# An encoder block with 32 experts: one 1 MB weight chunk brought in 16 transfers of 8 partitions each

## The chip, the cores and the metric

The kernel runs on one core of a Trainium2 chip. The metric is the time of one execution on the device in microseconds (us); lower is better. The input is one sequence of 256 tokens with a width of 1024, all in float32.

## What is computed

One encoder layer: RMSNorm, a combined projection, three token mixers (neighbourhood attention, dilated windows, attention to a memory), their gated merge with a residual, and then the expert stage, in which the change lies. Each token goes to 4 of 32 experts. Cut to what matters:

```python
logits = h @ router_w + router_b
top_val, top_idx = lax.top_k(logits, 4)
top_w = softmax(top_val)
# per expert e, for the tokens xb that chose it:
gu = xb @ w_gu[e] + b_gu[e]              # w_gu[e]: 1024 x 2048
g = minimum(gu[:, :1024], 7.0)
u = clip(gu[:, 1024:], -7.0, 7.0)
a = (u + 1.0) * (g * sigmoid(1.702 * g))
y = a @ w_dn[e] + b_dn[e]                # w_dn[e]: 1024 x 1024
# x += sum over the chosen experts of top_w * y, then a last RMSNorm
```

## The kernel before, in words

The front (the mixers) takes about the first quarter of the time. Then all 32 experts are worked through in order, each with a block of up to 64 gathered tokens; tokens beyond that would go through an overflow loop. Each expert's weights, 12 MB, are read once from the chip's main memory and used once.

**Chunks and the ring.** Weights come in chunks of 1 MB: 128 partitions x 8 KB (CHUNK = 2048 floats). An expert has 12 (EXPERT_CHUNKS): chunks 0 to 7 are gate/up, 8 to 11 down. They lie in a ring of 20 slots (RING) in the arena, chunk c in slot c % 20. In the source, a partition's part of one gate/up chunk is one piece of 8 KB, and neighbouring chunks follow each other, so that a transfer of m chunks has one run of m x 8 KB in each partition.

**The order of the transfers** is worked out by transfers() (lines 156 to 171). Each entry is (expert, first chunk, number of chunks). Experts 4 to 30 take the list long, (0, 4) and (4, 4): two transfers of 4 MB for gate/up. Down comes as two transfers of 2 MB. The first three experts and the last take smaller ones, and expert 6 has a list of its own with four transfers of 1 MB, because three of its chunks are put at other places (LENT). In the order, the gate/up chunks of expert n stand ahead of the down chunks of expert n - 1.

**Who issues.** SP issues all transfers, in the loop at lines 543 to 554: before each it waits until TensorE has used the chunks that lay in the slots (line 546), then load_weights (line 443) issues one transfer, at line 450, which raises the semaphore of its ring slot by 16.

```python
sp.wait_ge(chunk_used, NF + c - RING + m)
load_weights(*TRANSFERS[c], ring_slot(c))
```

**Who waits.** TensorE goes through an expert at lines 948 to 994: a small product for the bias, then the gate/up products of chunks 0 to 7 (gate_up, matmuls of line 591), between them the scatter of the expert before last and the transposes of line 898 (after chunk 3) and the gathering of later tokens (after chunk 5), then the down products of expert n - 1 and the transposes of line 904. Ahead of the first chunk of each transfer it waits in weights_landed (line 932) until the semaphore of the slot has come to 16 for each fill so far; fills_through (line 400) counts the fills. All matmuls are recorded at line 591, all weight transfers at line 450. gate_up and down raise chunk_used after each chunk.

VectorE and ScalarE take the products out of PSUM and compute the activation; GpSimd has no work in this stage.

Of the kernel before, what the change touches and what calls it, by code (L numbers as in the profile page):

```python
# [25 lines left out]
P = 128  # L26
# [13 lines left out]
EXPERTS, TOP_K = 32, 4  # L40
# [7 lines left out]
CHUNK = 2048  # L48
# [7 lines left out]
EXPERT_CHUNKS = 12  # L56
# [42 lines left out]
FIRST_LONG = 4  # L99

LENT_TO = 6
LENT = tuple(EXPERT_CHUNKS * LENT_TO + j for j in (1, 2, 3))

QK_DONE, QKV_DONE = {"C": 6, "A": 10, "B": 18}, {"C": 6, "A": 12, "B": 21}
# [41 lines left out]
def gate_up_chunk(n):  # L146

    return EXPERT_CHUNKS * n - 4 if n else 0
# [7 lines left out]
def transfers():  # L156

    short, long, down = [(j, 2) for j in range(0, KC, 2)], [(0, 4), (4, 4)], [(KC, 2), (KC + 2, 2)]
    end_down = [(KC, 2), (KC + 2, 1), (KC + 3, 1)]
    first_down = [(KC, 1), (KC + 1, 1), (KC + 2, 2)]  # L160
    order = [(0, 0, 2), (0, 2, 2), (0, 4, 2), (0, 6, 1), (0, 7, 1)]
    for n in range(1, EXPERTS):
        lent = [(0, 4), (4, 1), (5, 1), (6, 1), (7, 1)]
        order += [(n, *t) for t in (lent if n == LENT_TO else long if FIRST_LONG <= n < EXPERTS - 1 else short)]
        order += [(n - 1, *t) for t in (first_down if n == 1 else down if n < EXPERTS - 1 else end_down)]
    order += [(EXPERTS - 1, *t) for t in end_down]
    c, out = 0, {}
    for e, j, m in order:
        out[c] = (e, j, m)
        c += m  # L170
    return out


TRANSFERS = transfers()


# [4 lines left out]
def build(nc, t):  # L181
# [4 lines left out]
    w_gu = t["expert_w_gate_up"].rearrange("l e (p a) c -> (l e) p (a c)", p=P)  # L186
# [5 lines left out]
    with ExitStack() as ctx:  # L192
# [3 lines left out]
        def sem(name):  # L196
            return ctx.enter_context(nc.semaphore(name))
# [25 lines left out]
        ring = arena[:, 0:RING * CHUNK].rearrange("p (r c) -> p r c", r=RING)  # L223
# [105 lines left out]

        landed = [sem(f"landed{i}") for i in range(RING)]  # L330
        lent_in = {c: sem(f"lent_in{c}") for c in LENT}
        sums_open, overflow_added = sem("sums_open"), sem("overflow_added")
        first_in, t5_in_done, consts_in = sem("first_in"), sem("t5_in_done"), sem("consts_in")
        mem_in = [sem(f"mem_in{i}") for i in range(T)]
# [47 lines left out]
        def ring_slot(c):  # L382

            return c % RING

        def front_fills(r):

            return len(range(r - FRONT_SLOT, NF, FRONT_RING)) if FRONT_SLOT <= r < FRONT_SLOT + FRONT_RING else 0

        x_flat = x[:].rearrange("p t c -> p (t c)")  # L390
        bias_flat = bias_raw[:].rearrange("p b c -> p (b c)")
        lent_pieces = {LENT[2]: [behind_work[:, 512 * i:512 * (i + 1)] for i in range(4)],
                       LENT[0]: [bias_flat[:, 0:512], bias_flat[:, 512:1024], until_ranked[:], until_routed],
                       LENT[1]: [x_flat[:, 512 * i:512 * (i + 1)] for i in range(4)]}

        def piece(c, i):

            return lent_pieces[c][i] if c in LENT else ring[:, ring_slot(c), 512 * i:512 * (i + 1)]

        def fills_through(c):  # L400

            return front_fills(ring_slot(c)) + sum(ring_slot(b) == ring_slot(c) for b in TRANSFERS if b <= c and b not in LENT)

        ALL_CHUNKS = EXPERTS * EXPERT_CHUNKS

        def overflow_fills(j):

            return front_fills(ring_slot(j)) + sum(ring_slot(c) == ring_slot(j) for c in TRANSFERS if c not in LENT) + 1

        def by_row(dst, tt):  # L410

# [30 lines left out]
        def _(sp):  # L442
            def load_weights(e, j, m, r):

                if j < KC:
                    src = w_gu[bass.ds(e, 1), :, j * CHUNK:(j + m) * CHUNK].rearrange("o p c -> (o p) c")
                else:
                    first = (j - KC) % 2 * CHUNK
                    src = w_dn[bass.ds(e, 1), :, (j - KC) // 2, first:first + m * CHUNK].rearrange("o p c -> (o p) c")
                sp.dma_start(ring[:, r:r + m, :].rearrange("p r c -> p (r c)"), src).then_inc(landed[r], 16)  # L450

            def lend(c, first, n, place):

                e, j, _ = TRANSFERS[c]
                src = w_gu[bass.ds(e, 1), :, j * CHUNK + 512 * first:j * CHUNK + 512 * (first + n)].rearrange("o p c -> (o p) c")
                sp.dma_start(place, src).then_inc(lent_in[c], 16)
# [5 lines left out]
            for i in range(NF):  # L462
# [7 lines left out]
                kind, n = FRONT[i]  # L470
                dst = raw_of(i)
                if i in WIDE_FIRST or i in WIDE_LAST:
                    late = int(i in WIDE_LAST)
                    first = (n - late) * SLOTS_W
                    src = {"mem": w_mem, "in": w_in}[kind][:, 4 * late:4 * late + 4, first:first + 2 * SLOTS_W]
                    dst = dst.rearrange("p (k c) -> p k c", k=4)
                elif kind in ("mem", "in", "out"):
                    src = {"mem": w_mem, "in": w_in, "out": w_out}[kind][:, :, n * SLOTS_W:(n + 1) * SLOTS_W]
                    dst = dst.rearrange("p (k c) -> p k c", k=KC)
                elif kind == "branch_b":  # L480
                    src, dst = w_br[kind], dst.rearrange("p (k c) -> p k c", k=2)
                else:
                    src, dst = w_br[kind][:, :, n * 512:(n + 1) * 512], dst.rearrange("p (k c) -> p k c", k=4)
                if i == 0:
                    sp.dma_start(dst[:, 0:KC // 2], src[:, 0:KC // 2]).then_inc(first_half_in, 16)
                    dst, src = dst[:, KC // 2:], src[:, KC // 2:]
# [56 lines left out]
            for c, (_, _, m) in TRANSFERS.items():  # L543
                if c < RING or c in LENT:
                    continue
                sp.wait_ge(chunk_used, NF + c - RING + m)
                load_weights(*TRANSFERS[c], ring_slot(c))
                if c == RING:
                    sp.wait_ge(routed, 1)
                    lend(LENT[0], 3, 1, until_routed)  # L550
                if c == gate_up_chunk(LENT_TO + 2):
                    assert c - RING + m > LENT[1]
                    sp.dma_start(b_dn, t["expert_b_down"].rearrange("l e c -> (l e) c")).then_inc(b_dn_in, 16)
                    sp.dma_start(final_g, bass.AP(t["final_norm_g"].tensor, 0, [[0, P], [1, D]])).then_inc(final_g_in, 16)
# [34 lines left out]
        def _(pe):  # L589
# [342 lines left out]
            def weights_landed(c):  # L932

                if c in LENT:
                    pe.wait_ge(lent_in[c], {LENT[0]: 48, LENT[1]: 16, LENT[2]: 16}[c])
                else:
                    pe.wait_ge(landed[ring_slot(c)], 16 * fills_through(c))

            def down_products(n, bank):

                pe.wait_ge(aT_ready, n + 1)
                for j in range(KC, EXPERT_CHUNKS):
                    c = down_chunk(n) + j - KC
                    if c in TRANSFERS:
                        weights_landed(c)
                    down(ring_slot(c), j, bank)

            for n in range(EXPERTS):
# [10 lines left out]
                for k in range(KC):  # L959
                    c = gate_up_chunk(n) + k  # L960
# [49 lines left out]
            with pe.If(0 < n_over):  # L1010
                with pe.Fori(0, MAX_OVERFLOW) as b:
                    with pe.If(b < n_over):
                        n = b + EXPERTS
                        pe.wait_ge(P_ready, b + (EXPERTS // 2 + 1))
                        for half in range(2):

                            pe.wait_ge(XT_ready, b * 2 + (EXPERTS + half))
                            gather_half(half, BLK)
                        pe.wait_ge(XT_ready, b * 2 + (EXPERTS + 2))
                        pe.wait_ge(pick_ready, b + (EXPERTS + 1))  # L1020
                        pe.wait_ge(gu_drained, n + 1)
                        bias_rows(1)
                        for k in range(KC):
                            if k % 2 == 0:
                                pe.wait_ge(landed[ring_slot(k)], (b + overflow_fills(k)) * 16)
                            gate_up(lambda i: piece(k, i), k, XT[:, 0, :, 0:BLK])
                            if k == 3:
                                pe.wait_ge(PW_ready, n + 1)
                                turn_weights()
                        pe.wait_ge(WT_ready, n + 1)  # L1030
                        pe.wait_ge(act_ready, n + 1)
                        turn_act()
                        pe.wait_ge(aT_ready, n + 1)
                        for j in range(KC, EXPERT_CHUNKS):
                            if j % 2 == 0:
                                pe.wait_ge(landed[ring_slot(j)], (b + overflow_fills(j)) * 16)
                            down(ring_slot(j), j, 3)
                        pe.wait_ge(y_ready, n + 1)
                        scatter(1, overflow_added)
# [587 lines left out]
```

## Time and profile before

| | |
|---|---|
| median of 3 runs | 1218.38 us (1218.35 to 1219.38) |
| the profiled execution | 1214.18 us |
| its span, first to last instruction | 1212.4 us |
| mean granted TensorE clock | 0.989 |
| TensorE busy | 1162.4 us, 96% |
| moved by DMA | 455.15 MB, mean 375 GB/s |

The profile is that of one execution; times inside it are counted from the start of its span. PE is TensorE, SP the engine that issues the transfers (SPq its queue). A wait is put down to what came last. Busy TensorE time includes the time in which a matmul waits inside the array's pipeline, so 96% is not 96% of the peak.

### The profile page before, as it was taken

The page shows a single profiled execution, that of the slowest core. Times are in us where ns is not written, and L with a number is a line of the kernel's source. Part 1 is how long each engine was busy: PE and PEld are TensorE (multiplying, and loading weights), DVE is VectorE, ACT ScalarE, POOL GpSimd, SP SyncE. Part 2 cuts the span into 40 slices and gives each one's busy share as a digit, 9 for nine tenths or more (in the row PEclk, how much of TensorE's full clock was granted, in tenths as well). Part 3 has the DMA queues.
Part 4 walks back from the last instruction along what each step waited for, and adds up shares of the span by engine and source line. Part 5 has one row for each costly group of instructions (what it writes and reads, how often), then busy time and mean ns, then how long its engine had stood idle before and what let it go on. Part 6 is the DMA issues. An engine that isn't in the chain of part 4 may idle for free.

```text
span 1212.4 us, 14185 instructions
## 1 busy us (share of the span) xinstructions
PE 1162.4 (96%) x6145; PEld 594.1 (49%) x6145; DVE 247.1 (20%) x511; ACT 269.5 (22%) x579; POOL 206.5 (17%) x89
## 2 busy tenths in 40 slices
PE   8999999999999999999999999998899989989996
PEld 8989877898434333333343333333333333333332
DVE  3136122233321121111111211111111111111112
ACT  6457567445110111001011100100000000000002
POOL 5865757785000000000000000000000000000000
PEclk9999999999999999999999999999999999999999
DMA  8766645587999999999999999999999999999995
GB/s 287 261 243 217 203 144 172 211 282 266 429 429 425 431 431 435 415 434 432 430 431 432 431 432 432 433 432 431 431 432 432 431 431 432 431 431 430 432 430 240
DMA packets 62136, 455.15 MB, mean 375 GB/s; under 512 B 5129, under 2 KB 33705, under 8 KB 43512
## 3 DMA queue, kind: packets, MB, share of 16 engines
q1 hardware_dynamic: 62072, 454.22, 90.5%
q8 instruction: 50, 0.82, 0.2%
q14 instruction: 14, 0.11, 0.0%
HBM read 453.13 MB, written 1.07 MB: 375 GB/s over the span
## 4 chain that ended last, share of the span: by engine, by line
PE 65%; DMA 30%; ACT 2%; DVE 1%; POOL 1%; issue 0%; DVEq 0%; SPq 0%; ACTq 0%; POOLq 0%
PE ps L591 62%; DMA arena<-in_expert_w_gate_up 26%; DMA arena<-in_expert_w_down 3%; PE ps L904 1%; PE ps L646 1%; PE ps L898 1%; ACT arena L1104 1%; POOL w_lowc L580 0%; ACT arena L1094 0%; POOL w_lowa L580 0%; DMA arena<-in_mem 0%; DVE arena L1394 0%; ACT L1118 0%; DVE arena L1398 0%; DVE arena L1406 0%
## 5 line engine op out<-in xcount | busy, mean ns | idle before, releaser
L591 PE MATMUL ps<-arena,gathered_T 128*64 128x512 f32 x2034 | 469.4, 609 | 31.8 <-DMA arena<-in_expert_w_gate_up 31.8
L591 PE MATMUL ps<-arena 128*64 128x512 f32 (+6 forms) x1490 | 316.4, 562 | 2.2 <-DMA arena<-in_expert_w_down 1.3
L591 PEld LDWEIGHTS ps<-arena,gathered_T 128*64 128x64 f32 x2034 | 144.3, 139 | 296.3 <-issue 269.3
L591 PEld LDWEIGHTS ps<-arena 128*64 128x64 f32 (+3 forms) x1490 | 113.4, 149 | 194.9 <-issue 192.3
L1227 ACT COPY arena<-ps 128x256 f32<-128x256 f32 x32 | 11.9, 372 | 350.2 <-PE ps L898 350.2
L1506 DVE TENSOR_SCALAR arena<-arena 128x128 f32<-128x128 f32 x64 | 19.3, 344 | 306.9 <-PE ps L898 306.9
L1512 DVE TENSOR_SCALAR arena<-ps 128x512 f32<-128x512 f32 x32 | 22.1, 692 | 275.1 <-PE ps L591 275.1
L1218 ACT ACTIVATE gathered_T<-ps,g_cols 128x128 f32<-128x128 f32 x128 | 36.6, 368 | 172.9 <-PE ps L591 172.9
L591 PEld LDWEIGHTS ps<-arena,x_normed 128*128 128x128 f32 x512 | 59.5, 191 | 24.8 <-issue 24.3
L591 PE MATMUL ps<-arena,x_normed 128*128 128x128 f32 x512 | 65.4, 281 | 0.2 <-DVE arena L1463 0.2
L1237 ACT COPY arena<-ps 128x512 f32<-128x512 f32 x31 | 18.2, 586 | 172.2 <-PE ps L591 172.2
L1521 DVE COPY arena<-ps 128x512 f32<-128x512 f32 x32 | 22.1, 692 | 154.9 <-PE ps L904 154.9
L580 POOL TENSOR_TENSOR w_lowa<-arena,w_high 128x1024 fp32r<-128x1024 f32 x20 | 48.9, 2470 | 22.8 <-ACT w_high L1074 13.7
L580 POOL TENSOR_TENSOR w_lowc<-arena,w_high 128x1024 fp32r<-128x1024 f32 x20 | 48.6, 2451 | 20.3 <-ACT w_high L1074 20.3
L580 POOL TENSOR_TENSOR w_lowb<-arena,w_high_odd 128x1024 fp32r<-128x1024 f32 x20 | 48.0, 2423 | 22.4 <-ACT w_high_odd L1074 22.4
L580 POOL TENSOR_TENSOR w_lowd<-arena,w_high_odd 128x1024 fp32r<-128x1024 f32 x20 | 47.5, 2399 | 19.1 <-ACT w_high_odd L1074 19.1
L1074 ACT CAST w_high_odd<-arena 128x1024 fp32r<-128x1024 f32 x40 | 39.9, 1047 | 32.8 <-PE ps L591 32.7
L1074 ACT CAST w_high<-arena 128x1024 fp32r<-128x1024 f32 x38 | 37.9, 1046 | 41.1 <-PE ps L591 41.0
L1231 ACT ACTIVATE arena<-arena 128x512 f32<-128x512 f32 x32 | 20.3, 633 | 108.8 <-DVE arena L1512 108.8
L591 PE MATMUL ps<-w_high_odd,h_T_parts 128*128 128x256 f32 (+1 forms) x240 | 41.5, 322 | 0.0
L591 PEld LDWEIGHTS ps<-w_high_odd,h_T_parts 128*128 128x128 f32 x240 | 34.5, 188 | 5.3 <-issue 1.4
L904 PEld LDWEIGHTS ps<-ident,arena 128*128 128x128 f32 x128 | 17.8, 208 | 26.0 <-issue 26.0
(229 smaller groups left out, 895.7 us busy)
## 6 DMA issues: line engine op xcount, KB each, us to landing
arena<-in_expert_w_gate_up SPq DMA_DIRECT2D x53, 4096.0 KB, 38.5
arena<-in_expert_w_down SPq DMA_DIRECT2D x61, 2048.0 KB, 38.6
arena<-in_expert_w_gate_up SPq DMA_DIRECT2D x19, 2048.0 KB, 10.6
arena<-in_w_in SPq DMA_DIRECT2D x29, 1024.0 KB, 5.1
arena<-in_expert_w_down SPq DMA_DIRECT2D x6, 1024.0 KB, 38.6
arena<-in_expert_w_gate_up SPq DMA_DIRECT2D x4, 1024.0 KB, 7.0
arena<-in_w_out SPq DMA_DIRECT2D x4, 1024.0 KB, 5.8
arena<-in_w_mem_kv SPq DMA_DIRECT2D x3, 1024.0 KB, 11.4
```

The source lines that it names most:

```text
L580: last = nc.gpsimd.tensor_tensor(low_of(i)[:, half], raw_of(i)[:, half], high_of(i)[:, half].bitcast(F32), ALU.subtract)
L591: return nc.tensor.matmul(out, lhsT, rhs, start=start, stop=stop, **kw)
L646: last = nc.tensor.transpose(ps[:, 6 + hh, kt * S + tt * P:kt * S + (tt + 1) * P], scores[:, u % 4, hh, tt, kt * P:(kt + 1) * P], ident[:])
L898: last = nc.tensor.transpose(ps[:, 3, tt * P:(tt + 1) * P], PW[:, tt, :], ident[:])
L904: last = nc.tensor.transpose(ps[:, 2, f * P:(f + 1) * P], sig.rearrange("p (q f) -> p f q", f=4)[:, f, :], ident[:])
L1074: nc.scalar.copy(high_of(i)[:, half], raw_of(i)[:, half]).then_inc(high_ready, 1)
L1218: last = nc.scalar.mul(xt[:, c, 0:width], ps[:, bank, k * P:k * P + width], g_cols[:, 3 * KC + c:3 * KC + c + 1])
L1231: nc.scalar.activation(sig, gate_c, ACT.Sigmoid, scale=ALPHA).then_inc(sig_ready, 1)
L1237: nc.scalar.copy(y_sb, ps[:, bank, :]).then_inc(y_ready, 1)
L1506: last = vec.tensor_scalar(PW[:, tt, :].rearrange("p (a s) -> p a s", a=2), bcast(slots, 1, 2), key_tile[:, tt, e], w_sel[:, tt, e], ALU.i ...
L1512: vec.tensor_scalar(gate_c, ps[:, 0, :], LIMIT, None, ALU.min).then_inc(gate_ready, 1)
L1521: vec.tensor_copy(aT, ps[:, 2, :].rearrange("p (f s) -> p f s", f=4)).then_inc(aT_ready, 1)
```

## The change

The second gate/up transfer of expert 24, (4, 4), becomes (4, 3) and (7, 1). The second of these, the last gate/up chunk (number EIGHTHS = 12 * 24 + 3 = 291), isn't brought by load_weights but by 16 transfers, each over 8 partitions with 8 KB in each, 64 KB. They raise a semaphore of their own, 256 in all, and TensorE waits for 256. The counts of fills of the ring slot leave this chunk out. Nothing else is changed.

```diff
+EIGHTHS_OF = 24
+EIGHTHS = EXPERT_CHUNKS * EIGHTHS_OF + 3
...
         lent = [(0, 4), (4, 1), (5, 1), (6, 1), (7, 1)]
-        order += [(n, *t) for t in (lent if n == LENT_TO else long if FIRST_LONG <= n < EXPERTS - 1 else short)]
+        eighths = [(0, 4), (4, 3), (7, 1)]
+        order += [(n, *t) for t in (lent if n == LENT_TO else eighths if n == EIGHTHS_OF else long if FIRST_LONG <= n < EXPERTS - 1 else short)]
...
+        eighths_in = sem("eighths_in")
...
-            return front_fills(ring_slot(c)) + sum(ring_slot(b) == ring_slot(c) for b in TRANSFERS if b <= c and b not in LENT)
+            return front_fills(ring_slot(c)) + sum(ring_slot(b) == ring_slot(c) for b in TRANSFERS if b <= c and b not in LENT and b != EIGHTHS)
...
                 sp.wait_ge(chunk_used, NF + c - RING + m)
-                load_weights(*TRANSFERS[c], ring_slot(c))
+                if c == EIGHTHS:
+                    e, j, _ = TRANSFERS[c]
+                    for p in range(0, P, 8):
+                        src = w_gu[bass.ds(e, 1), p:p + 8, j * CHUNK:(j + 1) * CHUNK].rearrange("o p c -> (o p) c")
+                        sp.dma_start(ring[p:p + 8, ring_slot(c), :], src).then_inc(eighths_in, 16)
+                else:
+                    load_weights(*TRANSFERS[c], ring_slot(c))
...
                 if c in LENT:
                     pe.wait_ge(lent_in[c], {LENT[0]: 48, LENT[1]: 16, LENT[2]: 16}[c])
+                elif c == EIGHTHS:
+                    pe.wait_ge(eighths_in, 16 * (P // 8))
                 else:
                     pe.wait_ge(landed[ring_slot(c)], 16 * fills_through(c))
```

## Rows read from the trace of the kernel before

**Rows 1.** The page's 40 slices of the span: TensorE and the DMA rate.
```profile
PE   8999999999999999999999999998899989989996
DMA  8766645587999999999999999999999999999995
GB/s 287 261 243 217 203 144 172 211 282 266 429 429 425 431 431 435 415 434 432 430 431 432 431 432 432 433 432 431 431 432 432 431 431 432 431 431 430 432 430 240
```

**Rows 2.** Busy time in a stretch of 100 us ahead of the first waits.
```profile
core 0: us, PE busy (x) PEld busy (x) DVE busy (x) ACT busy (x) POOL busy (x), PEclk, DMA share, GB/s
600.00:700.00 100.00, 100.00 (x478) 38.03 (x474) 17.02 (x39) 10.36 (x27) 0.00 (x0) 1.00 1.01 433
```

**Rows 3.** The chain, one expert, early: start, length, what.
```profile
361.88 0.37 PE ps L898 x2
...
388.34 0.37 PE ps L898 x2
```

**Rows 4.** TensorE's waits for transfers (total us, times, longest), whole span, then from 860 us.
```profile
PE ps L591 <- DMA arena<-in_expert_w_gate_up: 31.8, 25, 2.3
...
PE ps L591 <- DMA arena<-in_expert_w_gate_up: 19.4, 15, 2.3
```

**Rows 5.** TensorE's instructions in order of time, the last experts.
```profile
1141.62 8.78 PE L591 MATMUL ps<-arena,gathered_T 128*64 128x512 f32 x32 [2.26 <-DMA arena<-in_expert_w_gate_up]
1185.38 7.09 PE L591 MATMUL ps<-arena 128*64 128x512 f32 x32 [1.29 <-DMA arena<-in_expert_w_down]
```

**Rows 6.** Around the changed transfer: its issue, the chain, TensorE, SP's next issues.
```profile
933.37 0.33 SPq L450 DMA_DIRECT2D arena<-in_expert_w_gate_up  x1
...
933.37 42.66 DMA arena<-in_expert_w_gate_up
...
976.08 3.65 PE L591 MATMUL ps<-arena,gathered_T 128*64 128x512 f32 x16 [0.98 <-DMA arena<-in_expert_w_gate_up]
979.66 2.05 PE L591 MATMUL ps<-arena,x_normed 128*128 128x128 f32 x16
981.65 3.65 PE L591 MATMUL ps<-arena,gathered_T 128*64 128x512 f32 x16
...
941.98 3.76 SPq L450 DMA_DIRECT2D arena<-in_expert_w_down  x2
```

**Rows 7.** Two stretches in which expert 6's transfers of 1 MB are moved.
```profile
440.00:455.00 15.00, 15.00 (x78) 6.06 (x78) 3.41 (x7) 2.15 (x6) 0.00 (x0) 1.00 1.00 426
455.00:470.00 15.00, 15.00 (x72) 5.29 (x70) 2.08 (x8) 0.96 (x2) 0.00 (x0) 1.00 1.02 440
```

**Rows 8.** Issue times in ns and landing in us: weights, bias, output.
```profile
L450 SPq DMA_DIRECT2D arena<-in_expert_w_gate_up x75: 327/328/584, 44.6 to 1138.3; - x75
...
L525 SPq DMA_DIRECT2D bias_raw<-in_expert_b_gate_up x4: 580/599/732, 295.6 to 297.7; - x4
DMA to landing us min/median/max: 2.7/3.0/9.2
...
DMA to landing us min/median/max: 2.6/2.7/2.8
```

**Rows 9.** The page's packets and its transfers with rows of 8 KB or more.
```profile
DMA packets 62136, 455.15 MB, mean 375 GB/s; under 512 B 5129, under 2 KB 33705, under 8 KB 43512
q8 instruction: 50, 0.82, 0.2%
q14 instruction: 14, 0.11, 0.0%
arena<-in_expert_w_gate_up SPq DMA_DIRECT2D x53, 4096.0 KB, 38.5
arena<-in_expert_w_down SPq DMA_DIRECT2D x61, 2048.0 KB, 38.6
arena<-in_expert_w_gate_up SPq DMA_DIRECT2D x19, 2048.0 KB, 10.6
...
arena<-in_expert_w_down SPq DMA_DIRECT2D x6, 1024.0 KB, 38.6
```

More of the change, by code:

```diff
@@ L400, in fills_through @@
         def fills_through(c):
-            return front_fills(ring_slot(c)) + sum(ring_slot(b) == ring_slot(c) for b in TRANSFERS if b <= c and b not in LENT)
+            return front_fills(ring_slot(c)) + sum(ring_slot(b) == ring_slot(c) for b in TRANSFERS if b <= c and b not in LENT and b != EIGHTHS)
         ALL_CHUNKS = EXPERTS * EXPERT_CHUNKS
         def overflow_fills(j):
-            return front_fills(ring_slot(j)) + sum(ring_slot(c) == ring_slot(j) for c in TRANSFERS if c not in LENT) + 1
+            return front_fills(ring_slot(j)) + sum(ring_slot(c) == ring_slot(j) for c in TRANSFERS if c not in LENT and c != EIGHTHS) + 1
         def by_row(dst, tt):
```

## The prediction

> **What bounds the kernel now.** I read the page's slices first, then stretches of the expert stage, then the waits and the chain, and last the two queues around the edit. The reader is to see in the slices that TensorE and the DMA engines are both nearly full from about a quarter of the span on, and that the DMA rate stands at 430 to 435 GB/s there [rows 1]. So busy shares don't decide; the waits do. Up to about 700 us TensorE never waits for a transfer: a stretch of 100 us has 100 us of TensorE work [rows 2]. It needs 26.5 us for an expert (from one L898 group of the chain, at 361.88, to the next, at 388.34) [rows 3]. An expert brings 12 MB, 12 x 1024 x 1024 bytes = 12.58 million bytes, which takes 29.2 us at 431 GB/s. TensorE thus eats up the lead that the ring of 20 chunks gives it, and from then on it waits for gate/up transfers: all its waits for them come to 31.8 us in 25 waits, 19.4 us of that in 15 waits after 860 us [rows 4]. From there to the end the chain runs from one weight transfer to the next, and the last of them, a down transfer, lands at 1185 us with TensorE waiting 1.29 us [rows 5]. **The bound around expert 24 is the DMA stream**, and TensorE has 29.2 - 26.5 = 2.7 us to spare per expert.
>
> The transfer that is changed is the second gate/up one of expert 24, issued at 933.37 us and waited for until 976.04, 42.66 us later; TensorE stood still 0.98 us for it [rows 6]. It spends 4 MB at 431 GB/s = 9.7 us of its 42.7 us being moved; for the other 33 us it stands behind earlier ones. The queue is that deep, and it is never dry.
>
> **The change, part by part.** *The split of (4, 4) into (4, 3) and (7, 1).* No byte is added. The 3 MB part lands one chunk earlier, 1.05 MB / 431 GB/s = 2.43 us, which lets TensorE start chunk 4 earlier, but the end hangs on the bytes behind it: 0. The wait on the freed slots is split into one for 3 slots and one for the fourth: with 33 us of queue in front, 0. Elsewhere the kernel brings chunks as single 1 MB transfers (expert 6, the stretch 440 to 470 us), and the rate stays at 426 and 440 GB/s [rows 7], so the smaller size over all 128 partitions is no cost.
>
> *SP's 16 issues.* A weight transfer takes the queue 0.33 us to issue; the four loads of the bias took up to 0.73 [rows 8]. 16 of them are 5.3 to 11.7 us. Behind them on SP stand the two down transfers of expert 23, issued in this lap 8.6 us after the transfer in question (941.98) [rows 6]; so they go out between 0 and about 3.4 us late. Cover: 33 us of queued transfers. Cost 0; without that cover it would be those 3.4 us, once. TensorE's one wait for 256 instead of a ring slot's count costs nothing by itself. POOL has nothing in this stage.
>
> *The rows of each transfer.* This is the term that counts. Each packet is one partition's row: 53 transfers of 4 MB, 80 of 2 MB (61 of them down) and 12 of 1 MB with rows of 8 KB (six of w_down, four of w_gate_up, and two into x), times 128, are 18,560; with the 64 instruction packets of queues 8 and 14 that makes 18,624, and the page has 62,136 - 43,512 = 18,624 packets of 8 KB or more, exactly [rows 9]. Rows are not cut up. A transfer of 8 rows then has 8 packets, and at most 8 of the 16 engines work on it. The Trainium skill says the same and more (DMA: Bandwidth & Descriptors, section on why a DMA increments its semaphore by 16): it takes the largest count up to 16 that divides the outer dimension, on the lowest-numbered engines, so all 16 pieces would go to the same 8. No view here shows which engine a packet ran on.
>
> If it is the same 8 each time (another 8 now and then would make it less), each of them carries 16 rows of 8 KB (131 KB) where it would have carried 8 (66 KB). At 431/16 = 27 GB/s per engine this is 4.86 us instead of 2.43: **+2.4 us** on these 8. The other 8 go on to later transfers, but every later transfer has rows on all 16, so it lands with the late ones, and at a stream that is full to the end they don't catch up. That is the lower end for a loss, if the eight are as late as the rest before it; if they are ahead of the others, part or all is hidden (down to 0).
>
> The upper side: the eight engines write to 8 neighbouring partitions at the same time, where the transfers of before spread over 128. The nearest rows are the four loads of the bias, 128 KB into 32 partitions each, beside the two halves of the output, 512 KB over 128 partitions: 2.7 to 3.0 us to landing against 2.6 to 2.8 [rows 8]. A quarter of the bytes in a quarter of the partitions isn't faster at all. Most of that is a fixed latency, so the rows allow both readings: time by bytes, or time by bytes per partition. Taken to the end, the second reading makes each piece as long as a 1 MB transfer over all partitions, 2.43 us, and the 16 in a row 38.9 us, +36.5. That is the far end, and it has no overlap between pieces. I take a middle case: neighbours in fours share a path into the memory with the rate of one engine. In step, four engines then need 4 x 8.2 KB / 27 GB/s = 1.21 us per piece, 19.4 us for 16, +17.0. But the engines are not held in step, since each goes to its next row as soon as it is done; with two at a time on a path it is 0.61 us per piece, 9.7 us for 16: **9.7 - 2.43 = +7.3 us**. I take this one, between +2.4 and +17, because the engines have run freely for 700 us and will be spread. The Trainium skill has such a rule (SBUF — State Buffer, section on the DMA port swizzle): four neighbouring partitions share one of 16 ports, and a load into partitions 0 to 3 was measured at 27.6 GB/s, about a port's limit. By that page the in-step estimate of +17 is right for engines in lockstep. No run here shows it.
>
> *What the delay does.* TensorE reaches chunk 7 of expert 24 about 7.5 us after chunk 4 (two chunks of 3.65 us together, 2.05 us of gathering, one chunk of 1.8) [rows 6]; with a landing of 3 MB 2.4 us earlier it gets there near 981 to 984 us, so a delay up to 5 us isn't even seen there but in the down products of expert 23 and at expert 25. TensorE's pause may lower its clock for a while, as after the waits of over 2 us, where 32 matmuls take 8.78 us instead of 7.09 [rows 5]: 1.7 us, which the spare 2.7 us per expert cover. The tail after 1185 us is the same. So the sum is the delay of the stream, +7.3 us.
>
> The profiled execution took 1214.18 us beside a span of 1212.4; the median of the runs is 1218.38, 4.2 us above. I put the difference on the median: 1218.38 + 7.3 = 1225.7. About 0.2% (2.4 us) is what a measurement of this kernel can tell from no change.
>
> **Rivals.**
> - *Only the double load of eight engines* (no shared path): +2.4 us, 1220.8, with 1220.2 to 1221.3 for the spread of the engines. For it: the rate of a single engine is all that the rows prove. Against it: the bias loads. It stands just on the border of 0.2%. Chance 0.25.
> - *In step on the shared path, or worse*: +12 to +36, about 1235. Against it: nothing keeps the engines together. Chance 0.10.
> - *Not slower*: the eight engines that carry the small rows are those ahead of the others. The place is the landing of each transfer, which goes by its last engine; the price is zero as long as their lead is larger than 2.4 us (alone) or 7.3 us (shared path), and from that point on the rest shows. Also here: small transfers that do spread over all engines after all. 1218.4. Against it: eight of sixteen being all early is unlikely. Chance 0.12.
> - *Each small transfer pays its latency in turn*: 16 x 2.7 us = 43 us, +40. Against it: the queue holds several transfers at once, and single 1 MB transfers keep the full rate [rows 7]. Chance 0.02.
> - *Faster*: an earlier chunk 4 moves TensorE ahead; but the stream sets the end. Chance 0.03.
>
> **How the numbers follow.** The forecast, +4 to +11 us, has 0.48. The time is 1225.7. The range 1218.2 to 1231.0 takes in the hidden case, the double load, the forecast with its own range (1222.4 to 1229.4) and the low edge of the in-step case; it leaves out the rest of that, the latency in turn and most of the faster case, some 0.15. Slower by over 0.2%: 0.48, half of the double load (0.12), 0.10 and 0.02, 0.72 in all. Within 0.2%: the other half of that rival, 0.13, and the hidden case, 0.12, 0.25 in all. Faster: 0.03.
>
> **What the profile would show.** Right: expert_w_gate_up issues with 16 more of 64 KB and one of 3 MB; one dip in the DMA rate right around 970 to 1000 us and 431 GB/s again behind it; TensorE's waits for transfers up by about 7 us in all, first at expert 23's down products or at expert 25, with every later event shifted by one and the same amount up to the tail. Only a double load: the same with 2.4. Wrong: no shift before the tail (hidden), a shift that grows or shrinks after expert 26 (then the stream isn't the bound I take it for), or a late issue of the down transfers with the DMA share falling to nothing (SP's issues matter).

## The result and the profile after

The changed kernel takes 1226.3 us (median of 5 runs, 1223.05 to 1226.69) against 1218.35 us for the kernel before on the same chips (5 runs, 1216.04 to 1219.38): ratio 1.0063, 95% interval 1.0047 to 1.0078, or 7.7 us, with 5.7 to 9.5 as its interval. It is slower, and forecast was 1225.7.

The profiled execution was the one of 1226.3 us, with a span of 1224.5 us, 12.1 us more than the span before. The first lines to read are the page's slices and its packets, which answer to [rows 1, 9]:

```profile
PE   8999999999999999999999999999999979899996
DMA  8776645687999999999999999999999999999994
GB/s 286 264 243 200 205 144 172 211 287 268 427 431 428 430 438 432 415 430 435 434 428 432 434 433 430 430 432 429 432 430 431 373 402 434 430 434 429 433 428 184
DMA packets 62392, 455.15 MB, mean 372 GB/s; under 512 B 5257, under 2 KB 33833, under 8 KB 43640
```

The reader is to see two slices of 373 and 402 GB/s where 430 stood, while the DMA digit stays 9: the engines were as busy as ever and moved less. The page has 256 packets more. 128 of them are data (a 4 MB transfer had 128 rows; now there are 128 of 24 KB and 128 of 8 KB), the other 128 are small, under 512 B (5257 - 5129): 16 transfers with 8 semaphore updates each. That is one for each engine that carries a part, so 8 engines carry each transfer. The Trainium skill's rule (DMA: Bandwidth & Descriptors, section Why a DMA increments its semaphore by 16 and not by 1), the largest divisor up to 16, agrees with this trace: 8.

Around the event, in stretches of 10 us (columns: stretch, its length, busy time of PE, PEld, DVE, ACT, POOL with counts, granted clock, DMA share, GB/s):

```profile
960.00:970.00 10.00, 7.77 (x36) 2.89 (x34) 2.71 (x7) 0.58 (x1) 0.00 (x0) 0.95 0.99 422
970.00:980.00 10.00, 9.86 (x40) 3.52 (x36) 0.10 (x1) 0.10 (x1) 0.00 (x0) 0.88 1.00 239
980.00:990.00 10.00, 9.19 (x48) 3.98 (x48) 0.64 (x3) 1.41 (x5) 0.00 (x0) 1.00 1.02 356
990.00:1000.00 10.00, 8.14 (x40) 3.10 (x38) 2.75 (x5) 1.22 (x2) 0.00 (x0) 1.00 1.03 442
```

239 GB/s with a DMA share of 1.00 (the change's small rows begin at 969.2 us). A double load on eight engines alone can't do this: it moves work among engines, but each engine goes on at its own rate. Over the 30 us the mean is 346 GB/s, so bytes for (431 - 346) x 30 / 431 = 5.9 us were not moved.

Then TensorE, in order of time, which answers to [rows 6], with the start of expert 24 and of expert 25:

```profile
965.84 0.72 PE L601 MATMUL ps<-bias_parts,pick 128*128 128x512 f32 x2
968.79 8.78 PE L601 MATMUL ps<-arena,gathered_T 128*64 128x512 f32 x32 [2.23 <-DMA arena<-in_expert_w_gate_up]
...
980.81 3.65 PE L601 MATMUL ps<-arena,gathered_T 128*64 128x512 f32 x16 [0.95 <-DMA arena<-in_expert_w_gate_up]
984.39 2.05 PE L601 MATMUL ps<-arena,x_normed 128*128 128x128 f32 x16
986.38 3.65 PE L601 MATMUL ps<-arena,gathered_T 128*64 128x512 f32 x16
990.79 3.65 PE L601 MATMUL ps<-arena 128*64 128x512 f32 x16 [0.76 <-DMA arena<-in_expert_w_down]
995.55 3.65 PE L601 MATMUL ps<-arena 128*64 128x512 f32 x16 [1.10 <-DMA arena<-in_expert_w_down]
999.13 0.75 PE L914 MATMUL ps<-ident,arena 128*128 128x128 f32 x4
999.64 0.71 PE L601 MATMUL ps<-bias_parts,pick 128*128 128x512 f32 x2
1005.20 9.42 PE L601 MATMUL ps<-arena,gathered_T 128*64 128x512 f32 x32 [4.85 <-DMA arena<-in_expert_w_gate_up]
...
1195.79 7.09 PE L601 MATMUL ps<-arena 128*64 128x512 f32 x32 [1.31 <-DMA arena<-in_expert_w_down]
```

For chunk 7 itself, brought in 16 parts, TensorE doesn't stop (986.38 holds chunks 6 and 7). It stops 0.76 and 1.10 us at the two down transfers of expert 23 and 4.85 us at expert 25. In the trace of before, the rows at the same places of the program are:

```profile
965.73 7.09 PE L591 MATMUL ps<-arena,gathered_T 128*64 128x512 f32 x32 [0.91 <-DMA arena<-in_expert_w_gate_up]
...
985.13 7.04 PE L591 MATMUL ps<-arena 128*64 128x512 f32 x32
...
995.42 7.09 PE L591 MATMUL ps<-arena,gathered_T 128*64 128x512 f32 x32 [2.11 <-DMA arena<-in_expert_w_gate_up]
```

Taken at waits that a landing ended in both traces: at expert 24's first chunk the changed kernel is 968.79 - 965.73 = 3.1 us late already, before anything that was changed. At expert 25 it is 1005.20 - 995.42 = 9.8 us late, and at the last down transfer 1195.79 - 1185.38 = 10.4 us [rows 5]. **The event thus cost 6.7 to 7.3 us in these two executions, and it was kept to the end.** The other 3.1 us are the difference of these two executions ahead of expert 24 (the profiled one of before was 4.2 us under its median), and 1.7 us of the difference of the spans lie behind the last down transfer.

SP and its queue, answering to [rows 6, 8]:

```profile
937.82 6.92 SPq L555 DMA_DIRECT2D arena<-in_expert_w_gate_up  x16
944.79 0.54 SPq L454 DMA_DIRECT2D arena<-in_expert_w_down  x1
```

Beside these views, the trace keeps two kinds of records that are used below. A packet record has the start, the duration and the size of one DMA packet, and not its engine. A landing record has the time of each update that an engine, or the issuing queue, makes to a transfer's semaphore.

### The profile page after: what moved, and what is told of

Same layout as the page of the kernel before. It is cut to its first block, busy times and chain, and to the rows that moved or that the text cites. A ratio compares the mean times of both kernels' runs of the same rounds, so it can differ in the third digit from the quotient of the medians.

```text
span 1224.5 us, 14201 instructions
## 1 busy us (share of the span) xinstructions
PE 1169.4 (96%) x6145; PEld 597.5 (49%) x6145; DVE 246.5 (20%) x511; ACT 269.6 (22%) x579; POOL 206.0 (17%) x89
## 2 busy tenths in 40 slices
DMA packets 62392, 455.15 MB, mean 372 GB/s; under 512 B 5257, under 2 KB 33833, under 8 KB 43640
## 4 chain that ended last, share of the span: by engine, by line
PE 62%; DMA 34%; ACT 2%; DVE 1%; POOL 1%; issue 0%; DVEq 0%; SPq 0%; ACTq 0%; POOLq 0%
PE ps L601 59%; DMA arena<-in_expert_w_gate_up 26%; DMA arena<-in_expert_w_down 7%; PE ps L914 1%; PE ps L656 1%; PE ps L908 0%; POOL w_lowc L590 0%; POOL w_lowa L590 0%; ACT arena L1116 0%; DMA arena<-in_mem 0%; ACT arena L1106 0%; ACT L1130 0%; ACT w_high L1086 0%; DVE x_normed L1574 0%; PE ps L652 0%
## 5 line engine op out<-in xcount | busy, mean ns | idle before, releaser
L601 PEld LDWEIGHTS ps<-arena,x_normed 128*128 128x128 f32 x512 | 59.5, 192 | 24.8 <-issue 24.3
L590 POOL TENSOR_TENSOR w_lowc<-arena,w_high 128x1024 fp32r<-128x1024 f32 x20 | 48.5, 2450 | 21.7 <-ACT w_high L1086 21.7
```

The source lines that it names most:

```text
L590: last = nc.gpsimd.tensor_tensor(low_of(i)[:, half], raw_of(i)[:, half], high_of(i)[:, half].bitcast(F32), ALU.subtract)
L601: return nc.tensor.matmul(out, lhsT, rhs, start=start, stop=stop, **kw)
```

## The experiments

Each experiment but one makes its edit at four experts (18, 21, 24, 27), so that a few us per event stand well above the spread of the runs. In all of them the list of these experts is (0, 4), (4, 3), (7, 1). In the runs that split the chunk by partitions its last part is issued by this loop, where PIECES differs (cut; waits as in the change). Where a run changes more, its lines are shown or told.

```diff
+PIECES = [slice(p, p + 8) for p in range(0, P, 8)]
...
+                    for rows in PIECES:
+                        src = w_gu[bass.ds(e, 1), rows, j * CHUNK:(j + 1) * CHUNK].rearrange("o p c -> (o p) c")
+                        sp.dma_start(ring[rows, ring_slot(c), :], src).then_inc(split_in[SPLIT[c]], 16)
```

The theories: **1**, four neighbouring partitions share one path (the forecast); **2**, nothing but the double load of eight engines; and, formed after the first four runs, **3**, a row written outside the partitions that its engine serves in a 128-row transfer (below: a foreign row) slows the stream.

All results, each against the runs of the kernel before on the same chip; us is the ratio times the median of before:

| run | transfers per chunk | us per run, ratio (95% interval) | per event |
|---|---|---|---|
| d4_whole | 1 of 128 partitions | +1.1, 1.0009 (1.0000 to 1.0019) | 0.3 |
| n4_cols8 | 8 of 128, 1 KB in each | +1.1, 1.0009 (0.9999 to 1.0019) | 0.3 |
| a4_rows8 | 16 of 8 neighbours | +30.8, 1.0253 (1.0236 to 1.0270) | 7.7 |
| b4_stride4 | 16 of 8, 4 apart | +33.2, 1.0273 (1.0254 to 1.0293) | 8.3 |
| c4_rows16 | 8 of 16 neighbours | +21.4, 1.0176 (1.0157 to 1.0195) | 5.4 |
| f4_rows32 | 4 of 32 | +22.4, 1.0184 (1.0163 to 1.0206) | 5.6 |
| g4_rows64 | 2 of 64 | +24.3, 1.0200 (1.0178 to 1.0223) | 6.1 |
| l4_lower | 16 of 8, 4 apart, all into 0 to 63 | +7.8, 1.0064 (1.0048 to 1.0081) | 1.9 |
| u4_upper | 16 of 8, 4 apart, all into 64 to 127 | +46.3, 1.0380 (1.0357 to 1.0403) | 11.6 |
| v4_near_low | 16 of 8 neighbours, all into 0 to 63 | +33.5, 1.0276 (1.0240 to 1.0311) | 8.4 |
| o4_guest | 1 of 128, and 16 single rows more | +32.3, 1.0265 (1.0250 to 1.0279) | 8.1 |
| e_early12 | the change, at expert 12 alone | +7.4, 1.0061 (1.0048 to 1.0074) | 7.4 |

**The change four times (a4_rows8).**

> The change made at four experts (18, 21, 24, 27) instead of one: four chunks each in 16 transfers of 8 neighbouring partitions. Theory 1, shared path: the delay of the stream seen once in the changed kernel (about 7 us) comes four times and adds up, +28 us (20 to 34). Theory 2, only the double load of eight engines: +2.4 us each, +10 us. If a delay were a loss of one place (the state in which expert 24 found the queue), the sum would be below 4 x 7.

Measured +30.8 us, 7.7 per event, which is the changed kernel's 7.7 over again. The delays add up; theory 2 alone (+10) is out.

**The control (d4_whole).** PIECES is left away, the chunk is one transfer.

> The control: at the same four experts the list is (0, 4), (4, 3), (7, 1), and the last chunk is one transfer over 128 partitions. Both theories: 0, within 2 us. If the split of the 4 MB transfer itself costs, it shows here, and is to be taken off the others.

Measured +1.1 us. The split of the 4 MB transfer costs 0.3 us per event, and by the interval not more than 0.6.

**Rows 4 apart (b4_stride4).**

```diff
+PIECES = [slice(q + r, q + r + 29, 4) for q in range(0, P, 32) for r in range(4)]
```

> As the run before, but the 8 partitions of a transfer lie 4 apart (0, 4, ... 28, then 1, 5, ... 29 and so on, within each 32). The same 16 transfers of 8 rows of 8 KB, the same issues, the same number of engines; only the neighbourhood differs. Shared path (neighbours in fours share one): the engines of one transfer don't meet each other, and what is left is the double load and some meeting with the other transfers' rows, 2.4 to 4.8 us per expert, +10 to +19 us in all. Only the double load: the same as with neighbours, whatever that run shows. SP's issues as the cause: also the same as with neighbours.

Measured +33.2 us, above the 10 to 19 of the shared path and no less than with neighbours. **The forecast's path that four neighbours share falls here**, since no two rows of one transfer lie in the same four. SP's 16 issues as the cause would also have given the same as with neighbours; l4_lower and n4_cols8 below speak against it. This run's windows around the second event show where the time goes (columns as above; the first 8 of the 16 transfers write partitions 0 to 63, the last 8 write 64 to 127):

```profile
885.00:890.00 5.00, 2.89 (x9) 0.83 (x9) 0.69 (x1) 0.00 (x0) 0.00 (x0) 0.73 0.96 411
890.00:893.00 3.00, 3.00 (x14) 0.94 (x12) 0.00 (x0) 0.00 (x0) 0.00 (x0) 0.89 1.07 412
893.00:896.00 3.00, 3.00 (x16) 0.84 (x12) 0.00 (x0) 0.00 (x0) 0.00 (x0) 1.00 1.04 219
896.00:899.00 3.00, 3.00 (x16) 1.19 (x16) 0.47 (x2) 0.37 (x1) 0.00 (x0) 1.00 1.03 240
899.00:902.00 3.00, 3.00 (x16) 0.76 (x12) 0.27 (x2) 0.00 (x0) 0.00 (x0) 1.00 1.01 221
902.00:905.00 3.00, 3.00 (x24) 2.31 (x24) 0.00 (x0) 0.91 (x4) 0.00 (x0) 1.00 1.00 306
905.00:910.00 5.00, 2.86 (x14) 0.53 (x10) 1.34 (x3) 0.86 (x2) 0.00 (x0) 1.00 0.99 419
```

The small rows begin near 890 us. The stream keeps its rate for the first 3 us of them and then falls to half at once, 219 GB/s. The records of the single packets say the same. At the first event, the first 45 of the 128 small rows take 309 ns each, which is the time of an undisturbed one; of the other 83, 58 take 580 to 650 ns. And not the small rows alone: in the worst three microseconds of that event each packet of the other transfers takes 2.0 to 2.1 times its usual time, the least of them 2.0. With one path for four writers some would have taken four times as long. What differs between the two halves is the partitions. Theory 3 comes from this.

**16 partitions (c4_rows16).**

```diff
+PIECES = [slice(p, p + 16) for p in range(0, P, 16)]
```

> Four chunks each in 8 transfers of 16 neighbouring partitions. All 16 engines get one row of each, so there is no double load. Only the double load: 0. Shared path: four engines still write through one path of four neighbours, 3 to 5 us per expert with engines out of step, +11 to +20 us in all.

Measured +21.4 us, where the double load says 0: **a loss of 5.4 us per event without any engine having more to carry** (16 updates for each of the 8 transfers in the landing records). The shared path had said 11 to 20, so this run alone doesn't speak against it. The difference to 8 neighbours, 7.7 - 5.4 = 2.3 us, agrees with the double load's 2.4.

**Where the rows are written (l4_lower, u4_upper).** Sources, sizes, number and order of the transfers are those of b4_stride4; only the destination of half of them is moved, to a free area at the end of the arena. These kernels leave out the upper (u4_upper: the lower) 64 rows of four chunks, which keep old weights.

```diff
+                        dst = ring[rows, ring_slot(c), :]
+                        if rows.start >= 64:                    # l4_lower
+                            dst = behind_work[slice(rows.start - 64, rows.stop - 64, 4), :]
...
+                        if rows.start < 64:                     # u4_upper
+                            dst = behind_work[slice(rows.start + 64, rows.stop + 64, 4), :]
```

> As the run with rows 4 apart, at four experts, and from the same source rows; but the rows of partitions 64 to 127 are written to partitions 0 to 63 of a free area (so the last gate/up chunk of these experts keeps old weights in its upper 64 rows: that part of the computation is changed). New theory 3: a row written outside the partitions that its engine serves in a 128-row transfer slows all 16 engines about twofold while it is under way; with rows 4 apart that holds for the upper half alone. Then nothing is slowed here and only the double load stays: 2.4 us per expert, +10 us in all, packets of 8 KB at 309 ns throughout. If the cause were the source side or the number of transfers, it stays as with rows 4 apart, +35 us.

> The mirror image: the rows of partitions 0 to 63 are written to partitions 64 to 127 of the free area (the last gate/up chunk of four experts keeps old weights in its lower 64 rows). Theory 3: all 16 transfers are now of the slow kind, so the slowing of the run with rows 4 apart (35 us less 10 for the double load, 25) about doubles: +50 to +60 us in all. Source side or number of transfers: +35 us as before.

Measured +7.8 and +46.3 us. That decides between source and destination: same bytes read, and 38.5 us between the two. u4_upper stays below the 50 to 60 expected: twice as many foreign rows cost less than twice the slowing (38.5 us beyond l4_lower, where b4_stride4 has 25.4). The windows of l4_lower, then of u4_upper, around the same event:

```profile
885.00:890.00 5.00, 5.00 (x26) 1.47 (x22) 0.00 (x0) 0.00 (x0) 0.00 (x0) 1.00 1.01 424
890.00:895.00 5.00, 5.00 (x24) 1.81 (x24) 0.74 (x3) 0.37 (x1) 0.00 (x0) 1.00 1.05 449
```

```profile
890.00:895.00 5.00, 5.00 (x26) 1.72 (x24) 0.00 (x0) 0.00 (x0) 0.00 (x0) 1.00 1.04 285
895.00:900.00 5.00, 3.91 (x18) 1.18 (x14) 0.73 (x3) 0.37 (x1) 0.00 (x0) 1.00 1.01 211
900.00:905.00 5.00, 3.11 (x10) 0.96 (x12) 0.00 (x0) 0.00 (x0) 0.00 (x0) 0.73 1.04 223
905.00:910.00 5.00, 5.00 (x30) 2.70 (x28) 0.00 (x0) 0.74 (x3) 0.00 (x0) 0.93 0.98 301
```

In l4_lower no dip is left; by the packet records its small rows take 309 ns from the lowest to the 90th percentile. With 16 issues for each chunk, as in the change, it also says that the issues are not the cause. So theory 2's term stands pure here, 7.8 us for four events. In u4_upper the rate is down for some 20 us.

**The far half or a foreign partition (v4_near_low).** 8 neighbours as in the change, but all in the lower half (the chunk's upper 64 rows keep old weights).

```diff
+                        if rows.start >= 64:
+                            dst = behind_work[rows.start - 64:rows.stop - 64, :]
```

> At four experts 16 transfers of 8 neighbouring partitions as in the change, but the rows of partitions 64 to 127 go to partitions 0 to 63 of the free area (the chunk's upper 64 rows keep old weights). All rows then lie in the lower half, as in the run with rows 4 apart and +8 us, but most rows lie with another engine's partitions. If what slows is the way to the other half of the memory: only the double load, +8 to +10 us. If it is any row outside the engine's own partitions (theory 3): slowed as in the run with 8 neighbours in both halves, +25 to +35 us.

Measured +33.5 us (interval 29 to 38), against +7.8 with rows 4 apart in the same half. Its windows around the first event:

```profile
795.00:800.00 5.00, 5.00 (x24) 1.88 (x22) 0.00 (x0) 0.00 (x0) 0.00 (x0) 1.00 0.97 270
800.00:805.00 5.00, 5.00 (x25) 1.53 (x21) 0.74 (x3) 0.37 (x1) 0.00 (x0) 1.00 1.03 293
805.00:810.00 5.00, 5.00 (x32) 2.84 (x32) 0.00 (x0) 1.14 (x4) 0.00 (x0) 1.00 1.00 360
```

So it isn't the way to the other half, and it isn't the eight engines as such. What fits all the runs is which engine writes which partition. One rival is left: these two runs differ in the rows that they read as well, and neighbouring source rows with destinations 4 apart were not tried. The slowing again falls on every transfer: in the worst three microseconds of each of the four events no packet of the other transfers takes under 1.5 times its usual time. The Trainium skill (DMA: Bandwidth & Descriptors, section The descriptor swizzle) gives the assignment for a transfer of 128 partitions, engine = 8 x (p >> 6) + ((p >> 2) & 7). By it, if the 8 rows of a transfer go to engines 0 to 7 in order, rows 0, 4, ... 28 all lie in their engine's own partitions, and of rows 0 to 7 only row 0 does. No view shows the engine of a packet, but these three runs are as this assignment has them.

**32 and 64 partitions (f4_rows32, g4_rows64).** PIECES with steps of 32 and of 64.

> Four chunks each in 4 transfers of 32 neighbouring partitions: two rows for each engine in each. Theory 3: most rows still lie outside the engine's own partitions, and 8 rows per engine are under way for as long as with 16 partitions, so about 5 us per expert again, +15 to +23 us. Cost per transfer: half of the run with 16 partitions, +11 us. The path shared by four neighbours, two engines at a time on it: 4 us per expert, +15 us.

> Four chunks each in 2 transfers of 64 partitions, four rows for each engine in each. Theory 3, if rows go to the engines in order (engine i has rows 4i to 4i + 3 of the 64): half of all rows lie outside an engine's own partitions (engines 8 to 15 in the lower transfer, 0 to 7 in the upper), each sharing with the owner. Slowing for some 3 to 5 us per expert, +10 to +20 us in all, no double load. If a transfer of 64 rows were dealt out as one of 128 is, each half would be carried by 8 engines with double load in turn, and nothing lost in the end: 0.

Measured +22.4 and +24.3 us. A cost per transfer would have gone down from 8 to 4 to 2 transfers; it went 21.4, 22.4, 24.3. The first is near the upper edge of what was expected of theory 3 (15 to 23), the second above it (10 to 20; its interval is 21.7 to 27.1). Theory 3 has the direction right and the size too low there; two transfers of 64 partitions are no better than 8 of 16.

**The number of transfers (n4_cols8).**

```diff
+                        src = w_gu[bass.ds(e, 1), :, j * CHUNK + rows.start:j * CHUNK + rows.stop].rearrange("o p c -> (o p) c")
+                        sp.dma_start(ring[:, ring_slot(c), rows], src)   # rows: 256 columns
```

> Control for the number of transfers and of SP's issues: four chunks each in 8 transfers over all 128 partitions, of 1 KB in each (8 x 128 KB). Theory 3: no row lies outside its engine's partitions; only packets of 1 KB are a little less efficient (46 ns for 1 KB instead of 309 for 8 KB: 64 per engine take 2.9 us instead of 2.5), so 0.5 us per expert, +2 us in all. If a transfer as such cost 0.7 us (23 us over 4 x 8 transfers of 16 partitions): +20 us or more.

Measured +1.1 us. Eight issues and eight completions cost at most 0.6 us per event by themselves (upper end of the interval) as long as each transfer spans all partitions.

**One foreign writer (o4_guest).** The chunk comes whole; 16 transfers of one row each go into partitions 64 to 79 of the free area. They are issued ahead of the chunk, not behind it as the expectation has it:

```diff
+                if c in SPLIT:
...
+                        sp.dma_start(behind_work[rows, :], src).then_inc(split_in[SPLIT[c]], 16)
                 load_weights(*TRANSFERS[c], ring_slot(c))
```

> At four experts the last gate/up chunk comes as one whole transfer, and behind it 16 transfers of one single row of 8 KB each, into partitions 64 to 79 of the free area, which nobody reads. A transfer of one row has one packet and so one engine, outside its own partitions. It asks whether one such engine slows all 16. If each such row slows everybody twofold: 16 x 0.31 us more for all, 5 us per expert, +20 us in all, and on the carrying engine 16 x 0.62 = 9.9 us per expert, +40. If it only meets the owner of those partitions: the carrying engine loses 16 x 0.31 = 5 us (alone) to 9.9 us, the owner some 2.5, all others nothing; in all between +8 (it was ahead at first and uses its lead of several us up) and +40. The speed of the other engines' packets meanwhile tells them apart: 2x or 1x.

Measured +32.3 us. Its windows around the second event:

```profile
892.00:897.00 5.00, 5.00 (x24) 1.66 (x22) 0.74 (x3) 0.37 (x1) 0.00 (x0) 1.00 1.04 395
897.00:902.00 5.00, 5.00 (x32) 2.78 (x30) 0.00 (x0) 0.60 (x3) 0.00 (x0) 1.00 1.05 390
```

While the single rows are under way, the other transfers' packets take 1.0 to 1.2 times their usual time from the median to the 90th percentile; in the worst three microseconds of each event every one takes at least 1.12 times. One engine with foreign rows thus slows everybody a little, by an eighth to a sixth, not twofold. The carrying engine is the one that is late: over the second event, against the landing records of d4_whole at the same places, the last update falls back by 9.6 us and the others by about 1.0. That is 9.6 / 16 = 0.60 us per row, where a row alone takes 0.31. The whole run is +32.3 us, or 32.3 / 64 = 0.50 us per row, as at the first event the last update falls back by 5.4 us only: the carrying engine had a lead there. This run says what a transfer of a single partition costs in a full stream: 8 KB have the price of 0.5 us, in which the stream moves 217 KB.

**An early expert (e_early12).** The change at expert 12 alone, where TensorE waits for no transfer in the kernel before.

> The change made at expert 12 instead of 24, in the stretch where TensorE never waits for a transfer. If the DMA stream is what sets the end from the start of the expert stage on (it is full there too), the delay of about 7.5 us is passed on unchanged: +6 to +9 us. If what TensorE doesn't wait for is hidden, 0. The changed kernel's own delay was +8 us.

Measured +7.4 us (5.8 to 9.0), the same as at expert 24. The small rows are moved from 620 to 634 us, and TensorE soon stands still, where it waits for nothing in the kernel before:

```profile
644.82 3.65 PE L602 MATMUL ps<-arena 128*64 128x512 f32 x16 [0.63 <-DMA arena<-in_expert_w_down]
654.50 9.67 PE L602 MATMUL ps<-arena,gathered_T 128*64 128x512 f32 x32 [4.88 <-DMA arena<-in_expert_w_gate_up]
```

So the work that TensorE had in store at expert 12 was smaller than the delay. The stream is the bound from expert 12 on at least, not only from 700 us on where TensorE's first waits stand; an earlier expert, with more in store, was not tried.

## Why the prediction came out right, and where it didn't

**Right: the bound and the passing on.** The DMA stream sets the end; a delay in it is kept (6.7 us at expert 25, 7.3 at the end); four events cost four times as much; at expert 12 as much as at 24. SP's 16 issues took 6.92 us, within the 5.3 to 11.7 reckoned, and the next transfer was issued at 944.79 without a gap in the stream. The split as such is nothing (d4_whole, n4_cols8).

**Right: eight engines and the double load.** 8 updates per transfer, and l4_lower has it alone, 1.9 us per event (interval 1.5 to 2.5) for the 2.4 of the sum. In l4_lower's landing records the last engine falls back by 2.3 to 2.6 us at each of the first three events. That the whole run comes to less than four times that may be because steps of single engines outside the eight no longer count once the eight are the last; it was not tried.

**Wrong: the step of the shared path.** The upper term was reckoned as neighbours in fours on a path of one engine's rate, two at a time, 9.7 - 2.43 = 7.3, the double load included. The size was right, 7.7 measured, the mechanism wasn't. Rows 4 apart should have cured it and didn't (8.3 per event), no packet was four times as long, and in the worst microseconds every packet was slowed alike. In its place stand two terms: 2.4 us of double load on eight engines, and about 5.4 us of slowing of all 16 (c4_rows16, which has only this term). Their sum is 7.8, an estimate, since the slowing is no constant: beyond the 1.9 of l4_lower, b4_stride4 has 6.4 and u4_upper 9.7 us per event. That the wrong mechanism gave the measured number is chance. It was near for 16 partitions too (11 to 20 expected of it, 21.4 measured), and failed for 32 (15 and 22.4) and for rows 4 apart (10 to 19 and 33.2).

**Wrong, without effect on the sum: the 3 MB part.** It was to land 2.4 us earlier. TensorE took it at 980.81 for 976.08, 4.7 us later, or 1.7 us later without the 3.1 from before the event, as the slowing fell on it as well.

The Trainium skill (SBUF — State Buffer, section on the DMA port swizzle) speaks of ports shared by four neighbouring partitions. Ports are perhaps what lies behind the slowing; that was not shown. The prediction's in-step estimate, +17, was not seen, nor a slowing far above twofold in the bulk of the packets: in the worst three microseconds the median was 2.0 to 2.1 times the usual time in b4_stride4 and u4_upper, and at most 2.4 in g4_rows64. Meeting on a shared place alone doesn't explain v4_near_low either, where all rows lie in the lower half and yet every packet under way was at 1.5 times or more.

**Wrong: TensorE's waits.** "Up by about 7 us in all" was said. They answer to [rows 4], whole span (the wait for w_down was 1.3 us before):

```profile
PE ps L601 <- DMA arena<-in_expert_w_gate_up: 33.8, 29, 4.9
...
PE ps L601 <- DMA arena<-in_expert_w_down: 3.2, 3, 1.3
```

2.0 and 1.9 us more, 3.9 in all. The whole span mixes in what differs ahead of the event, so take it from expert 24's first chunk on, that wait left out: there the waits went from 14.3 to 18.8 us, 4.5 more, and up to the last down transfer TensorE's busy time went from 205.4 to 208.2 us, 2.9 more. Together that is 7.4 us, the delay of the event. So a good third of the delay stands as slower matmuls: after the wait of 4.85 us the 32 matmuls took 9.42 us, for 7.09 at the same place before, with a granted clock of 0.50 (1.2 GHz) in the first 3.8 us of them. A wait's cost is not to be read from the sum of waits. Nor do the 8.78 us that the prediction took after waits of over 2 us hold at each of them: before, the wait of 2.11 us at 995.42 is followed by 7.09. The shift at the start of the experts isn't one constant either, as had been said: 7.0 us at expert 25 (999.64 against 992.60), 11.5 at expert 26. It is constant only where it is taken at landings.

**Open.** Why engines that write foreign rows slow all 16 engines, a single one by an eighth to a sixth and eight of them about twofold. The runs show that it hangs on the destination (l4_lower, u4_upper) and that it lasts as long as such rows are under way. They don't show the part of the chip in which it happens, nor the engine of any row; that the rule is "outside its own partitions" is the reading that fits them all.

## What to carry to other kernels

Where the transfers are the bound, as here, bring each chunk over all 128 partitions; cut it along the columns if it must be cut (8 pieces, +0.3 us), not along the partitions (5.4 to 8.3 us for 1 MB, which takes 2.4). The cost falls on every transfer under way, and it is kept to the end of the stream; it was so at expert 12 as well, ahead of TensorE's first wait. A DMA share of 1.0 with half the GB/s is the sign to look for.

## What was not expected of the hardware

Two transfers of 64 partitions each cost 6.1 us more than one of 128, although every engine should have the same number of rows and bytes: both have 16 updates in the landing records.

The 16 engines are far apart in a long stream. In the landing records of the kernel before, the first and the last engine's update of one transfer came 2.3 us apart at about 470 us and 6.4 us apart at 1200 us, and the distance grows in steps: now and then a single engine falls behind by about 1.5 us, mostly a few us after one of the 16 KB packets of the instruction queue (50 of them in the page). That these packets are the cause was not tried. As each transfer lands with its last engine, such a step counts in full once it hits the engine that is last, as in the changed kernel near 1035 us, where the last update falls back by 1.6 us. In the changed kernel this gap was 6.4 us before the event and 8.9 us after: the first update lost 5.0 us and the last 7.4. Which of the engines these are, no record shows.
